# Delta rule scan: another order of the head of a step, with the next step's Gram products behind each state product

## The reference

```python
    gcum = jnp.cumsum(gc, axis=-1)
    decay = jnp.exp(jnp.where(tril, gcum[..., :, None] - gcum[..., None, :], -jnp.inf))
    kb = kc * bc[..., None]
    lower = jnp.where(strict, jnp.einsum('nbhid,nbhjd->nbhij', kb, kc) * decay, 0.0)
    rhs = jnp.concatenate([vc * bc[..., None], kb * jnp.exp(gcum)[..., None]], axis=-1)
    sol = lax.linalg.triangular_solve(eye + lower, rhs, left_side=True, lower=True, unit_diagonal=True)
    attn = jnp.where(tril, jnp.einsum('nbhid,nbhjd->nbhij', qc, kc) * decay, 0.0)

    def step(S, inp):
        v_new = u_i - jnp.einsum('bhck,bhkv->bhcv', w_i, S)
        o = (jnp.einsum('bhck,bhkv->bhcv', q_i * jnp.exp(g_i)[..., None], S)
             + jnp.einsum('bhij,bhjv->bhiv', a_i, v_new))
        S = (S * jnp.exp(g_last)[..., None, None]
             + jnp.einsum('bhck,bhcv->bhkv', k_i * jnp.exp(g_last[..., None] - g_i)[..., None], v_new))
```

## Time and profile before

| | |
|---|---|
| median of 3 runs | 4660.02 us (4655.83 to 4677.4) |
| the profiled execution | 4661.97 us |
| its span, first to last instruction | 4660.2 us |
| busy: PE, DVE, ACT, POOL | 4062.3, 2013.0, 926.6, 435.7 us |
| the two scans together | 549 us of the span |
| a later step of a scan | 44.5 us |

### The profile page before, as it was taken

How to read it: one execution, slowest core, us unless ns; L and a number is a source line. 1 busy time by engine, 2 the same in 40 slices (tenths; PEclk the granted TensorE clock), 3 DMA queues, 4 the chain that set the end, 5 groups by cost and what they waited for, 6 DMA issues and landing times. The chain is left out here.

```text
span 4660.2 us, 71311 instructions
## 1 busy us (share of the span) xinstructions
PE 4062.3 (87%) x30658; PEld 2761.8 (59%) x30658; DVE 2013.0 (43%) x3601; ACT 926.6 (20%) x2129; POOL 435.7 (9%) x454
## 2 busy tenths in 40 slices
PE   5988898889699996989999957777798999898998
PEld 3567757777244444577598722222346887547877
DVE  2655455555422212364374541111325445465445
ACT  2422232231100003153163110000232000252000
POOL 0022102310011110032040001111000000000000
PEclk8989998999799998989999979999899999999999
DMA  5400140002699993100101279999111222221221
GB/s 194 175 25 2 56 163 20 2 19 95 249 385 387 386 394 113 55 19 19 54 1 55 82 284 394 390 391 387 65 55 59 76 88 86 72 76 57 90 90 50
DMA packets 236504, 659.55 MB, mean 142 GB/s; under 512 B 15697, under 2 KB 33054, under 8 KB 236190
## 3 DMA queue, kind: packets, MB, share of 16 engines
q1 hardware_dynamic: 221598, 634.01, 36.1%
q0 software_dynamic: 14592, 20.98, 2.2%
HBM read 631.88 MB, written 23.07 MB: 141 GB/s over the span
## 5 line engine op out<-in xcount | busy, mean ns | idle before, releaser
L713 PE MATMUL bank<-hT_b,weight_ring 128*128 128x384 f32 x1792 | 590.0, 489 | 2.7 <-PEq L178 2.1
L713 PEld LDWEIGHTS bank<-hT_b,weight_ring 128*128 128x128 f32 x1792 | 337.8, 191 | 248.9 <-issue 24.4
L2800 PE MATMUL bank<-weight_ring,xs_b 128*32 128x512 f32 x2640 | 314.7, 629 | 64.2 <-DMA weight_ring<-in_moe_w_up 58.0
L2800 PE MATMUL bank<-weight_ring_extra_b,xs_b 128*32 128x512 f32 x2480 | 275.3, 594 | 31.3 <-DMA weight_ring_extra_b<-in_moe_w_up 31.3
L2800 PEld LDWEIGHTS bank<-weight_ring,xs_b 128*32 128x32 f32 x2640 | 83.8, 115 | 269.8 <-issue 182.3
L2033 PE MATMUL bank<-mixed_b,swiglu_sums_b 128*128 128x256 f32 x1056 | 236.9, 381 | 5.8 <-DVE swiglu_sums_b L2080 5.8
L2857 ACT ACTIVATE moe_silu_b<-bank 128x256 f32<-128x256 f32 x80 | 25.5, 383 | 1003.3 <-PE bank L2800 1003.3
L2868 DVE TENSOR_SCALAR xs_b<-bank,factor_b,mod_b 128x64 f32<-128x64 f32 (+1 forms) x384 | 95.5, 323 | 296.0 <-PE bank L2783 296.0
L2033 PEld LDWEIGHTS bank<-mixed_b,swiglu_sums_b 128*128 128x128 f32 x1056 | 201.7, 191 | 34.2 <-issue 6.5
L2800 PEld LDWEIGHTS bank<-weight_ring_extra_b,xs_b 128*32 128x32 f32 x2480 | 78.6, 110 | 206.4 <-issue 176.1
L2769 POOL DMA_INDIRECT residual<-moe_out_b,slot_row_parts x80 | 124.0, 1550 | 730.5 <-DVE moe_out_b L2882 715.9
(11 more groups left out here) (514 smaller groups left out, 7325.4 us busy)
## 6 DMA issues: line engine op xcount, KB each, us to landing
weight_ring_extra_b<-in_moe_w_down SPq DMA_DIRECT2D x34, 2048.0 KB, 25.8
weight_ring<-in_moe_w_gate SPq DMA_DIRECT2D x66, 1024.0 KB, 16.4
weight_ring<-in_moe_w_up SPq DMA_DIRECT2D x66, 1024.0 KB, 20.0
weight_ring_extra_b<-in_moe_w_gate SPq DMA_DIRECT2D x62, 1024.0 KB, 17.5
weight_ring_extra_b<-in_moe_w_up SPq DMA_DIRECT2D x62, 1024.0 KB, 19.0
weight_ring<-in_moe_w_down SPq DMA_DIRECT2D x30, 2048.0 KB, 23.7
weight_ring<-in_ada_w SPq DMA_DIRECT2D x24, 2048.0 KB, 8.2
weight_ring<-in_ssd_w_in SPq DMA_DIRECT2D x12, 2048.0 KB, 7.9
```

Source lines behind the costliest of these rows:

```text
L713: last = pe.matmul(acc, w[:, k, c * P:(c + 1) * P], hT[:, k, h * half:(h + 1) * half], start=(k == 0), stop=(k == KT - 1))
L2800: last = pe.matmul(in_bank(g)[lanes[c], :], xs[:, e % 2, kt, g * GROUP:(g + 1) * GROUP], w[:, k, :, c * COLS:(c + 1) * COLS], start=(kt == 0),
```

## The change

The diff changes the order in `delta_scan`, and the waits with it. It adds and removes no arithmetic.

- TensorE: the `gram` products of step s + 1 are made in step s, each right behind the `state` product of its own direction; those of step 0 ahead of the loop. `qk` stays at the head of a step. `turn1` goes behind `kturn` and `ks` of both directions.
- VectorE: the decayed Gram blocks become a function `lower`, called right behind the state update of the same direction. `uv1` goes ahead of `u1`, behind `attn` of its direction. `beside` has one operation for each direction at each of the levels 1, 2, 4, 8 and 16: `eks`, `rest`, `kend`, `rb`, `qs`.
- POOL: the triangle masks go behind the masks of levels 1 and 2.
- TensorE's level 2 waits for `u1` at its first products and for `uv1` at its second.

The core of the diff:

```diff
-    PEM = ["gram", "qk", "turn1", "kturn", "ks"]
+    PEM = ["gram", "qk", "kturn", "ks", "turn1"]
...
-    BESIDE = {2: ["eks", "rest"], 4: ["rb", "kend"], 8: ["qs"]}
-    DVM = ["ge", "low", "attn", "u1", "uv1"]
+    BESIDE = {2: ["rest"], 4: ["kend"], 8: ["rb"], 16: ["qs"]}
+    DVM = ["ge", "low", "attn", "uv1", "u1", "eks"]
...
-    POM = ["attn"] + [f"a{s}" for s in SMALL]
+    POM = ["a1", "a2", "attn"] + [f"a{s}" for s in SMALL[2:]]
...
         @block.gpsimd
         def _(pool):
-            for s in steps():
+            def attention(s):
                 for d in (FWD, BWD):
                     wait(pool, dvm[d], s, "attn")
...
+            for s in steps():
                 for n, size in enumerate(SMALL):
+                    if n == 2:
+                        attention(s)
                     for d in (FWD, BWD):
...
+            def gram(d, s):
+
+                cols = slice(chunk_cols(ORDER[d][s]), chunk_cols(ORDER[d][s]) + P)
+                if s:
+                    wait(pe, acm[d], s - 1, "new")
+                each(d, s, "gram", B[d][1], lambda h: kT[:, h, cols], lambda h: kT[:, h, cols])
+
             cumulated(0)
+            for d in (FWD, BWD):
+                gram(d, 0)
             for s in steps():
                 for d in (FWD, BWD):
...
                     if s:
                         wait(pe, dvm[d], s - 1, "out")
-                    each(d, s, "gram", B[d][1], lambda h: kT[:, h, cols], lambda h: kT[:, h, cols])
                     each(d, s, "qk", B[d][2], lambda h: kT[:, h, cols], lambda h: qT[:, h, cols])
                 for d in (FWD, BWD):
-                    wait(pe, pom[d], s, "a1")
-                    wait(pe, dvm[d], s, "ge")
-                    for h in range(GQ):
-                        for rows in halves:
-                            last = pe.matmul(small_bank(d, 1)[rows, h, :], A[rows, d, 0, h, :], unit[rows, :],
-                                             start=True, stop=True)
-                    last.then_inc(pem[d].sem, 1)
...
                     each(d, s, "ks", B[d][3], lambda h: kT[:, h, cols], lambda h: S[:, d, h, :])
+                for d in (FWD, BWD):
+                    wait(pe, pom[d], s, "a1")
+                    wait(pe, dvm[d], s, "ge")
+                    for h in range(GQ):
+                        for rows in halves:
+                            last = pe.matmul(small_bank(d, 1)[rows, h, :], A[rows, d, 0, h, :], unit[rows, :],
+                                             start=True, stop=True)
+                    last.then_inc(pem[d].sem, 1)
...
-                        wait(pe, dvm[d], s, f"uv{below}")
+                        wait(pe, dvm[d], s, "u1" if n == 1 else f"uv{below}")
...
                         wait(pe, acm[d], s, f"ct{size}")
+                        if n == 1:
+                            wait(pe, dvm[d], s, "uv1")
...
                     each(d, s, "state", B[d][3], lambda h: KE[:, d, h, :], lambda h: NW[:, d, h, :])
+                    if s + 1 < TT:
+                        gram(d, s + 1)
...
+            def lower(d, s):
+
+                t = ORDER[d][s]
+                wait(dve, acm[d], s, "decay")
+                wait(dve, pem[d], s, "gram")
+                if s:
+                    wait(dve, pom[d], s - 1, f"a{SMALL[-1]}")
+                    wait(dve, pem[d], s - 1, f"ct{TOP}")
+                for rows in halves:
+                    dve.tensor_tensor(L[rows, d], B[d][1][rows, :, rows], E[rows, d, :, rows], ALU.mult)
...
+            for d in (FWD, BWD):
+                lower(d, 0)
             for s in steps():
                 for d in (FWD, BWD):
...
                     wait(dve, pem[d], s, "qk")
                     dve.tensor_tensor(G[:, d], B[d][2], E[:, d], ALU.mult).then_inc(dvm[d].sem, 1)
-                for d in (FWD, BWD):
-                    wait(dve, pem[d], s, "turn1")
+                    wait(dve, pom[d], s, "a1")
                     if s:
                         wait(dve, pem[d], s - 1, "new")
...
+                for d in (FWD, BWD):
+                    wait(dve, pem[d], s, "turn1")
+                    dve.scalar_tensor_tensor(out=UW[:, d, 0], in0=small_bank(d, 1), scalar=-1.0, in1=over_small(unit[:]),
+                                             op0=ALU.mult, op1=ALU.add).then_inc(dvm[d].sem, 1)
+                for d in (FWD, BWD):
+                    beside(d, s, 1)
...
                     dve.tensor_tensor(S[:, d], S[:, d], B[d][3], ALU.add).then_inc(dvm[d].sem, 1)
+                    if s + 1 < TT:
+                        lower(d, s + 1)
```

More of the change, by code:

```diff
@@ L1247, in beside @@
                 cols = slice(chunk_cols(t), chunk_cols(t) + P)
-                if size == 2:
+                if size == 1:
+                    wait(dve, dvm[d], s, "attn")
                     wait(dve, pem[d], s, "ks")
@@ L1251, in beside @@
                         .then_inc(dvm[d].sem, 1)
+                elif size == 2:
                     wait(dve, dvm[d], s, "eks")
@@ L1262, in beside @@
                 elif size == 8:
+                    wait(dve, dvm[d], s, "rest")
+                    dve.tensor_tensor(R[:, d], R[:, d], wide(dec.beta, d, t), ALU.mult).then_inc(dvm[d].sem, 1)
+                elif size == 16:
                     wait(dve, acm[d], s, "rowexp")
@@ L1275, in _ @@
             dve.wait_ge(cleared, 2)
+            def lower(d, s):
[7 more added lines that the diff above has]
+                    dve.tensor_tensor(L[rows, d], B[d][1][rows, :, rows], E[rows, d, :, rows], ALU.mult)
+                rows, cols = far_rows(d)
+                dve.tensor_tensor(far[rows, d], B[d][1][rows, :, cols], E[rows, d, :, cols], ALU.mult) \
+                    .then_inc(dvm[d].sem, 1)
+                wait(dve, dvm[d], s, "ge")
+                beta = dec.beta[:, t, d, h0:h0 + GQ].unsqueeze(2).to_broadcast([P, GQ, TOP])
+                dve.tensor_tensor(L[:, d], L[:, d], beta, ALU.mult)
+                dve.tensor_tensor(far[rows, d], far[rows, d], beta[rows], ALU.mult).then_inc(dvm[d].sem, 1)
@@ L1293, in _ @@
                     wait(dve, pem[d], s, "qk")
                     dve.tensor_tensor(G[:, d], B[d][2], E[:, d], ALU.mult).then_inc(dvm[d].sem, 1)
-                for d in (FWD, BWD):
-                    wait(dve, pem[d], s, "turn1")
+                    wait(dve, pom[d], s, "a1")
                     if s:
                         wait(dve, pem[d], s - 1, "new")
-                    dve.scalar_tensor_tensor(out=UW[:, d, 0], in0=small_bank(d, 1), scalar=-1.0, in1=over_small(unit[:]),
-                                             op0=ALU.mult, op1=ALU.add).then_inc(dvm[d].sem, 1)
-                    wait(dve, pom[d], s, "a1")
@@ L1307, in _ @@
                         wait(dve, pem[d], s, f"uv{size}")
-                        wait(dve, dvm[d], s, f"uv{size // 2}")
+                        wait(dve, dvm[d], s, "u1" if size == 2 else f"uv{size // 2}")
                         if size == TOP:
```

23 lines of the change are left out of this document (2 added, 21 removed).

## The result

| | before | after |
|---|---|---|
| median | 4662.6 us (4655.83 to 4677.4) | 4588.84 us (4585.84 to 4607.07) |
| ratio | | 0.9846, 95% interval 0.9811 to 0.9881 |
| profiled execution, its span | 4661.97, 4660.2 us | 4588.75, 4587.0 us |
| the two scans, from the state's clearing to its last update | 272.2, 271.0 us | 231.0, 229.8 us |

The change saves 73.8 us where 98.4 were forecast. The median of 4588.84 us is 27 us above the predicted 4562 and 1.2 us inside the upper end of the range, 4590. The windows of after that answer to the earlier trace rows: both scans, then a step of 36.86 us and one of 38.41 us.

A forecast was written before the change was run, and what follows sets the result against it. It took a chain through four engines in the two scans as the bound, TensorE waiting 5.0 us a step for POOL's masks. 6.6 + 1.55 = 8.15 us a step, 98.4 over both scans, gave 4562 us, range 4549 to 4590.

The forecast's parts named there:

- the head: Start of a scan step, up to level 2 on TensorE: reordering its pieces was to save 6.6 us a step.
- The backward output: Sign in a step's start: this product comes 4.1 us behind the forward output, without a wait for TensorE.
- the turn: TensorE's turning of the level-1 blocks: it was to be reached without a pause, 9.7 us behind the forward output.
- VectorE's end of the backward Gram: VectorE finishes the backward decayed Gram block at 414.24, with the forward output at 406.00 (8.24 us).
- no wait of the turn for POOL over 1 us: Sign: TensorE's level-1 turn no longer waits long for POOL's level masks, which cost 5.0 us each time before.
- rival (d): VectorE's uv operations run free of POOL: 8 us more saved, 4554 and below; chance 0.05 for 4545 to 4552.
- so I take 3.11 for all: 1.07 + 0.48 = 1.55: Levels 2 to 16 of a step: each takes 3.11 us with two VectorE operations behind it, saving 1.55 us.
- rival (a): Level 4 waits for POOL's mask, 1.5 us late: 18 us in all, 4580; chance 0.15 for 4574 to 4592.
- the granted clock at 1.00 throughout a step behind the first: Sign: TensorE runs at its full clock in every scan step after the first, with no stretch at 0.50.
- Rival (b): TensorE stays at 1.2 GHz in the levels: up to 26 us more a step; with half, 4718 us; chance 0.03.
- Rival (c): Behind the scans, a stage waiting for weights takes the gain back: 4660, or half of it; chance 0.03.

## Why the prediction was right in its direction and too large

**Right: the head.** The backward output came at 4.11 (forecast 4.1), the turn at 9.70 (9.7), VectorE's end of the backward Gram at 8.23 (8.24), no wait of the turn for POOL over 1 us. The term of 6.6 measured 7.04: the uv operation behind the mask took 0.41 to 0.63 us (median 0.51), not its 0.70 of before. That is part of rival (d), 5 us in twelve steps, and it pushed the other way. Undone one at a time the parts cost 3.9 us a step (POOL's order, with the clock that it brings), 1.76 (the turn) and 0.33 (Gram). They make 6.0 and not 7.04; each is the price with the other two in place, so they need not add up. The higher clock in the head is part of the gain: alone, in the kernel before with its wait filled, it gave 1.7 us.

**Wrong, first: "so I take 3.11 for all: 1.07 + 0.48 = 1.55".** The levels gave 0.63 us a step, 11 us less in twelve steps. The rows give 3.11 to levels 2 and 16 (the prediction says 2 and 8); that does not touch the sum, but both stand for something special, and two things were mis-sized.

The rhythm: in the traces of this study a level of 2 to 16 takes 3.11 only behind the turn or behind a level that was held up, and starts its two directions together (one group x32, as at 423.94 and 434.82). Left alone, the directions start 0.94 apart (326.57, 327.51) and a level takes 3.34. Without any collision the four take 13.12, 0.87 less than before.

The collision: `rest` beside POOL's masks takes 1.2 us each, two in 2.36, and this holds level 4 back. In the kernel before it took 0.69 us in all 24 cases, and the mask beside it was the one that got longer:

```profile
428.56 0.69 DVE L1253 TENSOR_TENSOR d_decay_b<-V_b,d_decay_b 128x512 f32<-128x512 f32 x1
428.75 1.08 POOL L1111 TENSOR_TENSOR d_level_b<-d_low_b,d_mask_b 128x256 f32<-128x256 f32 x1 [0.21 <-PE bank L1125]
```

The prediction priced that collision for POOL, in rival (a), and for VectorE's L1302, but not for `rest`, which the new table puts directly behind the update. The new table alone on the kernel before brings the same 1.2 us. The old table behind the new head has the collision too, and its levels 2 to 16 take 14.5 to 15.0 us, not 13.99; so the 0.63 is the sum of what the table gains and the new head costs there.

**Wrong, second: "the granted clock at 1.00 throughout a step behind the first".** The head got it; level 64 lost it in six of the twelve steps, 11 us in all in this trace and 22 in the next. Rival (b) was dismissed because the new head has no pause over 1 us and because short pauses in the levels had run at the full clock; but these had been read in steps whose head had already had its low stretch. The kernel before with its wait filled shows that it is enough to take the low clock out of the head for it to come at level 64. It is not needed: with the new table alone, the first step of each scan has both.

**Sum.** 12 x 0.92 of the levels and 11 us of the clock, less 5 of the head, are 17 us; the scans fell short of 98.4 by 16.0. Some 9 us more of the profile are the attention stage's clock, which differs as much between two executions of the kernel before. Rival (a) was there at a small size: level 2 took 3.35 and not 3.11, the mask of level 4 being late, and 3.11 where the attention masks were moved back; it cost nothing, as `rest` held the next level anyway. Rival (c) was not: no new wait for weights stands behind a scan. That the median lies in the range is luck. It lies in the part that was set aside for rival (a), between 4574 and 4592, and rival (a) did not bring it there; the levels, and a low clock at level 64 and in the attention stage, to which the forecast gave no term, did. The changed kernel once more had its median at 4597.59, outside.

**Open.** What decides whether a given step's level 64 falls, and what sets the clock in the attention stage; the runs show only that both change from run to run.

## What to carry to other kernels

Behind a chain through several engines, put ahead only what the next link reads: here the order of the masks on POOL was worth more (3.9 us a step) than the products moved over a step (0.33). Read a repeated stage's duration from a stretch where the neighbours are in the state they will have, and not from the fastest single case. Where small products and short waits follow each other on TensorE, try work that is due soon between them; here a wait filled with real work paid twice, by the clock and by 0.7 us less behind level 64. Then look where the clock falls instead: a filled wait in the kernel before moved the fall and gained nothing.

## What the hardware showed that was not expected

- TensorE's clock went to 1.2 GHz without an idle stretch: behind 3.0 us in which it was busy for 1.87 us and no wait was over 0.52 us. The same work in another step, busy for 1.89 us, kept it at 2.4 GHz. Two identity products in each of two such waits kept it there in all steps of that run.
- Taking the low clock out of one place can bring it at another: mended in the head of the kernel before, it came at level 64, and the time stayed within 0.3%.
- VectorE's `rest` (both inputs in SBUF) takes 2.36 us for two beside POOL's masks and 1.29 for two with POOL idle (397.02), while `eks` (one input in PSUM) takes 0.68 beside POOL's attention mask (316.88), and 0.67 to 0.68 in all 24 cases, each beside a mask. The Trainium skill, page "SBUF — State Buffer", section "SBUF: two separate sides", says that GpSimd and a VectorE operation with two SBUF inputs share one port pair, which the one that starts first holds to its end. The trace agrees: at 428.56 `rest` started first and the mask took 1.08, at 320.45 the masks were already running one behind another and `rest` took 1.2. In such a run of operations both pay: three small masks take 0.84 each in their new place (2.52 at 314.09), where four took 0.70 each before.
